# The query projection of a product-key expert layer run on the unscaled residual, the norm's root applied to the queries

## The reference, cut to what matters

```python
x = x + mixing_sublayer(rms_norm_2(x, norm1_g[l]), ...)
xn = rms_norm_2(x, norm2_g[l])           # x * rsqrt(mean(x^2) + eps) * g
q = (xn @ wq).reshape(t, 8, 2, 128)      # 8 heads, 2 halves of 128
scores = einsum('thcd,hcnd->thcn', q, sub_keys)      # 128 keys each
sv, si = top_k(scores, 16)               # then the best 16 of the 16 x 16 sums
gate = softmax(best_s); idx = ...        # 128 experts of 16384 for each token
act = gelu(xn . u_tab[idx]) * gate
x = x + sum(act * v_tab[idx])
```

## Time and profile before

| | |
|---|---|
| profiled execution | 2299.26 us |
| its span, first to last instruction | 2297.5 us |
| granted TensorE clock, mean | 0.972 |
| TensorE busy (matmul) | 2174.9 us, 95% |
| TensorE weight load | 1943.5 us, 85% |
| VectorE busy | 1213.2 us, 53% |
| ScalarE busy | 428.9 us, 19% |
| GpSimd busy | 473.3 us, 21% |
| DMA | 616.38 MB, mean 268 GB/s |
| chain that ended last | TensorE 76%, DMA 14%, VectorE 4% |

### The profile page before, as it was taken

How to read it: one execution, slowest core, us unless ns; L and a number is a source line. 1 busy time by engine, 2 the same in 40 slices (tenths; PEclk the granted TensorE clock), 3 DMA queues, 4 the chain that set the end, 5 groups by cost and what they waited for, 6 DMA issues and landing times.

```text
span 2297.5 us, 32593 instructions
## 1 busy us (share of the span) xinstructions
PE 2174.9 (95%) x13344; PEld 1943.5 (85%) x13344; DVE 1213.2 (53%) x2482; ACT 428.9 (19%) x1023; POOL 473.3 (21%) x410
## 2 busy tenths in 40 slices
PE   7999699998998999999999998998999999999998
PEld 4466488886677999999999998666899999999998
DVE  3254521112552796878744343552697878744433
ACT  3013310000241103433100000242112433100000
POOL 0000000000000013454433341000013445433341
PEclk9998799998998999999999998999999999999999
DMA  9145123433322388999999995423288999999996
GB/s 378 47 156 201 73 88 132 160 145 134 124 114 111 146 320 343 378 396 400 410 409 409 391 406 221 178 112 128 110 300 352 397 382 400 409 409 408 404 401 250
DMA packets 113525, 616.38 MB, mean 268 GB/s; under 512 B 10201, under 2 KB 10585, under 8 KB 95322
## 3 DMA queue, kind: packets, MB, share of 16 engines
q1 hardware_dynamic: 55578, 403.31, 44.8%
q0 software_dynamic: 57504, 208.82, 23.7%
q10 hardware_dynamic: 288, 2.10, 0.3%
HBM read 612.16 MB, written 2.03 MB: 267 GB/s over the span
## 4 chain that ended last, share of the span: by engine, by line
PE 76%; DMA 14%; DVE 4%; issue 2%; ACT 1%; POOL 0%; POOLq 0%; DVEq 0%; ACTq 0%; SPq 0%
PE psum L390 74%; DMA arena<-in_peer_v 8%; DMA arena<-in_peer_u,small 6%; PE psum L425 1%; PE psum L473 1%; DVE arena L1911 0%; DVE arena L1920 0%; POOL arena L2060 0%; ACT HT L1086 0%; DMA arena<-in_w_mod 0%; DVE arena L1935 0%; DVE rstd L1641 0%; DVE arena L1494 0%; POOLq L2028 0%; ACT arena L1237 0%
## 5 line engine op out<-in xcount | busy, mean ns | idle before, releaser
L390 PE MATMUL psum<-HT,arena 128*128 128x160 f32 (+1 forms) x5984 | 989.7, 326 | 14.5 <-DVE HT L1643 7.1
L390 PEld LDWEIGHTS psum<-HT,arena 128*128 128x128 f32 x5984 | 921.9, 191 | 66.7 <-issue 16.7
L390 PE MATMUL psum<-arena 128*128 128x160 f32 (+6 forms) x5850 | 873.0, 311 | 24.8 <-DMA arena<-in_peer_v 15.2
L390 PEld LDWEIGHTS psum<-arena 128*128 128x128 f32 (+2 forms) x5850 | 807.8, 191 | 75.1 <-issue 29.8
L1960 DVE SCALAR_TENSOR_TENSOR arena<-arena,small 128x1024 f32<-128x1024 f32 x180 | 231.3, 1285 | 289.0 <-DMA arena<-in_peer_v,small 288.6
L2060 POOL DMA_INDIRECT arena<-in_peer_u,small x192 | 248.8, 1296 | 310.5 <-DVE small L1911 268.9
L2060 POOL DMA_INDIRECT arena<-in_peer_v,small x192 | 210.6, 1097 | 361.5 <-PE psum L390 205.0
L1911 DVE CUSTOM_DVE_ANT_0 arena<-arena 128x1024 f32<-128x1024 f32 x192 | 229.1, 1221 | 58.7 <-DMA arena<-in_peer_u,small 57.2
L2066 POOL DMA_DIRECT2D row_tokens<-arena x2 | 1.2, 624 | 1067.6 <-ACT arena L960 1067.6
L390 PE MATMUL psum<-arena,HT 128*128 128x384 f32 (+3 forms) x544 | 199.7, 526 | 8.5 <-DVE HT L1643 7.0
L390 PEld LDWEIGHTS psum<-arena,HT 128*128 128x128 f32 x544 | 106.4, 198 | 93.5 <-issue 45.3
(11 more groups left out here) (228 smaller groups left out, 1004.6 us busy)
## 6 DMA issues: line engine op xcount, KB each, us to landing
arena<-in_peer_ut SPq DMA_DIRECT2D x64, 2048.0 KB, 10.8
arena<-in_peer_v SPq DMA_DIRECT2D x64, 2048.0 KB, 17.2
arena<-in_w_mod SPq DMA_DIRECT2D x12, 2048.0 KB, 9.7
arena<-in_w_in SPq DMA_DIRECT2D x16, 1536.0 KB, 6.2
arena<-in_w_up SPq DMA_DIRECT2D x11, 2048.0 KB, 8.1
arena<-in_peer_wq SPq DMA_DIRECT2D x8, 2048.0 KB, 7.2
arena<-in_w_out SPq DMA_DIRECT2D x6, 2048.0 KB, 7.3
arena<-in_w_down SPq DMA_DIRECT2D x11, 1024.0 KB, 4.8
```

The costliest lines, as they stand in the source:

```text
L390: return pe.matmul(o, a, b, start=start, stop=stop, skip_group_check=True)
```

## The change

A new region `XG` holds the residual times the norm's weight, without the root. VectorE fills it right behind the addition of each `lo` job. The query jobs read `XG` and wait for its semaphore `x_gained`. VectorE, and no longer ScalarE, takes the `pq` jobs out of PSUM, multiplying by the reciprocal root; `HT` is made in four products of 128x512 placed between the first four of them. TensorE waits for `HT` behind the last scores. The reads of all eight `pq` jobs stand in VectorE's program ahead of `choose(1, 0)`.

```diff
+        XG = view(wa_at + 16 * T, KC, T)
...
-                        channel_job(f"pq{2 * t + j}", w, HT, [j * 256, j * 256 + P],
-                                    ready=(s("l_normed"), KC) if t == 0 and j == 0 else None)
+                        channel_job(f"pq{2 * t + j}", w, XG, [j * 256, j * 256 + P],
+                                    ready=(s("x_gained"), 0) if t == 0 and j == 0 else None)
                         if t:
                             sub_scores(t - 1, 1 - j)
                 sub_scores(3, 1)
                 sub_scores(3, 0)
+                pe.wait_ge(s("l_normed"), KC + 4)
...
                 for t in range(4):
                     for j in range(2):
-                        m = 2 * t + j
-                        copy_out(f"pq{m}", QP[:, 2 * m:2 * m + 2, :],
-                                 bank(f"pq{m}")[:, :].rearrange("p (a t) -> p a t", a=2))
                         if t:
                             sub_scores(t - 1, 1 - j)
...
                     dve.tensor_tensor(x, ps[:, :].rearrange("p (a t) -> p a t", a=2), x, ALU.add
                                       ).then_inc(free(f"lo{g}"), 1)
-                for g in range(4):
                     jobs.wait_read(dve, f"lo{g}")
-                layer_norm(2, "n2g")
+                    for k in (2 * g, 2 * g + 1):
+                        dve.tensor_scalar(XG[:, k, :], XT[:, k, :], col2("n2g", k), None, ALU.mult
+                                          ).then_inc(s("x_gained"), 1)
+                mean_square("ls2", 0)
+                dve.wait_ge(s("l_rooted"), 2)
+                steps(dve.reciprocal(rstd[:, 0, :], rstd[:, 0, :]))
+                dve.wait_ge(s("x_gained"), KC)
+                for m in range(8):
+                    ps = reading(f"pq{m}")
+                    dve.tensor_tensor(QP[:, 2 * m:2 * m + 2, :], ps[:, :].rearrange("p (a t) -> p a t", a=2),
+                                      bc(rstd[:, 0, :].unsqueeze(1), P, 2, T), ALU.mult
+                                      ).then_inc(free(f"pq{m}"), 1)
+                    if m < 4:
+                        dve.tensor_tensor(HT[:, 2 * m:2 * m + 2, :], XG[:, 2 * m:2 * m + 2, :],
+                                          bc(rstd[:, 0, :].unsqueeze(1), P, 2, T), ALU.mult
+                                          ).then_inc(s("l_normed"), 1)
```

More of the change, by code:

```diff
@@ L305, in build @@
             "layer_params_in", "keys_in", "gate_in", "sb_wexp", "y2_done", "l_squared", "l_rooted",
-            "l_normed", "sbk_squared", "sbk_mean", "sbk_rooted", "sbk_ready", "sb_exp", "sb_spm", "sb_w",
+            "l_normed", "x_gained", "sbk_squared", "sbk_mean", "sbk_rooted", "sbk_ready", "sb_exp", "sb_spm", "sb_w",
             "ml_conv", "ml_exp", "ml_ready", "gate_ln", "gate_lf", "gate_a", "m_ready", "ml_d0", "ml_d",
```

## The result

The changed kernel took 2347.02 us (median of 4 runs, 2343.89 to 2350.77) against 2299.76 us before (median of 4, 2294.07 to 2305.45): ratio 1.0208, 95% interval 1.0187 to 1.0229, slower by 47 us. The forecast was 2345 us, within 2329 to 2361. The profiled execution took 2350.77 us, with a span of 2349.0.

What follows compares the result with a forecast made beforehand. TensorE, busy for 95% of the span, was taken as the bound. Selections later by 44.6 us, plus 6 for the clock, less 5 from value-tile waits, gave +45.6 us: 2345 us, range 2329 to 2361.

Steps and rivals of the forecast that it cites:

- The stall at the norm: TensorE's idle time between the sums of squares and the first query job, 3.53 us in each layer, goes.
- The lost clock of the first layer: Low granted clock (0.71) behind the first layer's second norm, costing 2.77 us up to the first query copy, goes.
- `XG` beside the sums of squares: VectorE's last two new products, 0.8 us, end before the sums of squares do; cost taken as nothing.
- The reads ahead of the choices: VectorE reads all eight query jobs before its first choice, which starts at 791.75 instead of 759.87 in the first layer.
- Selections later by 20.8 and 23.8 us: TensorE stands 27 us a layer for late gates, so its selection transposes start later, together 44.6 us.
- Terms behind the selections, +6 - 5: After the selections, 6 us lost to a low clock and 5 us given back from waits for value tiles.
- the part given back: Behind the selections, DMA catches up during TensorE's standing, so 5 us of its 15.2 us waits for value tiles go.
- The clock term: Low TensorE clock behind the idle time at the selections costs 3 us a layer, 6 in all.
- The ramp left out, as a rule has it: Leaving out the low clock's cost behind TensorE's idle time, as the Trainium skill advises, gives 2339 us.
- The third: Rival: first choices run between the query reads, so the delay is hidden; 9.8 us faster, 2289.5 us; chance 0.03.
- The second: Rival: all 15.2 us of waits for values go and the clock costs nothing; +29.4, 2329 us; chance 0.08.
- The first: Rival: the whole rest of each layer follows the late gates; 61.5 us slower, 2361 us; chance 0.07.
- The fourth: Rival: TensorE still waits at the first query job for keys or weights, leaving no difference; chance 0.02.

Runs made afterwards that it cites:

- gates_late_29: Kernel before plus 17 extra reciprocals of 128x256 on VectorE between the fourth and fifth choice, making the gates late; 2345.42 us, ratio 1.0208.
- before_select_25: Kernel before with the selections behind pair job 25 instead of 19 and the gated stretch from job 28 instead of 22; 2317.43 us, ratio 1.0087.
- after_kept_busy: Changed kernel plus 56 unused products a layer on TensorE ahead of its wait for the gates; 2346.74 us, ratio 1.0222 to the kernel before.
- after_again: The changed kernel run once more, unaltered, beside other runs on the same chip; 2347.12 us, ratio 1.0226 to the kernel before.
- reads_moved: Kernel before, only that VectorE instead of ScalarE copies out the eight query jobs, ahead of the first choice; 2355.68 us, ratio 1.0251.
- scores_scaled: Kernel before with queries from the unscaled residual, ScalarE still copying them out, and the root applied when it copies scores; 2285.95 us, ratio 0.9947.

## Why the prediction was right, by its steps

- **The stall at the norm goes.** As priced: no idle time before the first query job.
- **The lost clock of the first layer goes.** The first query job is read 7.21 us behind its start (739.69 - 732.48), where it was 9.95 before; 2.74 of the 2.77 us are gone. Both layers now take 177.19 and 177.12 us to the selections. That the second layer was spared before was a matter of the execution, though: in the five profiles that keep the stall of 3.5 us the clock behind it is 0.71 or 0.72 in the first layer each time, and in the second 1.00 in three, 0.69 in gates_late_29 and 0.81 in before_select_25.
- **`XG` beside the sums of squares.** The products took 0.35 us where 0.41 was taken, and the last two ended at 730.57, with 1.9 us to spare.
- **The reads ahead of the choices.** First choice 60.33 us behind the mean square of 732.68; forecast was 60.6 (791.75 - 731.19). The read took 0.69 us, the nearest row's value, not the strided one's 1.07.
- **Selections later by 20.8 and 23.8 us.** Measured 20.7 (177.19 - 156.50) and 23.4 (177.12 - 153.73), with 26.9 us of standing a layer where 27 was said.
- **Terms behind the selections, +6 - 5.** The sum +1 came out as +5.1, so this is the mis-sized term, and the mechanism of the part given back was wrong. I had 5 us come out of the waits for value tiles by the full DMA. Those waits did not fall, 15.1 and 15.5 us in the two profiles of the changed kernel against 15.2, so nothing was given back there. The clock term is real for TensorE, but taking it away gained nothing: after_kept_busy has the full clock and still +5.6, because TensorE then waits for the one-hot rows instead. So the two terms can't be added up as I did. What makes the +5.1 stays open. It came again in after_again (there 1.9 and 3.2 us by layers, here 0.3 and 4.7), but it is neither the stall nor the late gates and gathers as such, since reads_moved has all of these and shows -0.1. That the total lies 2 us from the forecast is in part luck: by the medians the loss was 47.3 us against 45.6, by the cut of this profile 49.1.
- **The ramp left out, as a rule has it.** Keeping TensorE at 1.00 behind the stall gained nothing. The Trainium skill's page "TensorE: Matmul & The Clock Gate", section "Part 1: The HAM clock gate (the "warmup" mystery)", puts the ramp at under 1% of a typical span and advises against fitting a specific number of slow products; without the term the sum gives 2339 us. The measured time lies 8 us above that. The trace agrees with the size: some 6 us of TensorE's work are 0.3% of the span, and by the kept-busy run they added nothing to the time. What the sum lacked without them was another thing of about the same size, which stays open as said.
- **The rivals.** The third, that the choices pass the waiting reads, is out: 8 reads with up to 7.11 us of idle time before each, and no choice between them. The second is out with the unchanged waits for tiles. The first, that the whole rest follows the gates, asked for 61.5 us and is out too: gates 30.2 us late in each layer cost 46.0 us in gates_late_29 (53.3 by the cut of its profile) and not 60. The fourth is out with the first query job's missing wait.

## What to carry to other kernels

When a read of PSUM moves from one engine to another, price where it stands in the new engine's program: an instruction of 0.69 us that waits for a late producer holds everything behind it, here eight choices by 32 us. Look for the slack between that engine's product and the bottleneck engine's wait for it (8.6 us here): lateness of 7.1 us inside it was free, and of 30.2 us all beyond it counted. A factor that is one number for each token can be applied where tokens lie on partitions and an engine copies anyway; here, in scores_scaled, that gave the gain without the loss.

## What the runs showed of the hardware

Half the clock behind a stall of 27 us cost TensorE some 3 us a layer of its own work (an estimate from some 6 us at 0.50) and the kernel nothing that these runs can tell: keeping TensorE at 2.4 GHz with useless products changed 2347.12 to 2346.74 us, and the profiled layers by 0.1 us or less, because other waits grew by 4.5 us.

A stall of 3.53 us at the same place brought the low clock behind it in some executions and not in others: in the second layer in two of five profiles. Where it did in full, the first query job was through in 9.9 us and not 7.2.

VectorE did not pass a waiting instruction: 16 reads in the two layers with up to 7.11 us of idle time before each, while later instructions of its program stood behind them.
